# First block of a two-block model: projections, three attentions and the output projection as one interleaved stage

## The chip, the cores and the metric

One core of one Trainium2 chip runs the whole program. The time is the device time of one execution in microseconds (us), inputs in the chip's memory, output written back. The kernel before: 1134.98, 1138.11 and 1143.31 us in three runs, median 1138.11.

## What is computed

The program has two blocks on a sequence of 256 tokens, 1024 features, float32. The change is in the first block, whose attention has three kinds of heads on one projection, and, apart from that, in a triangular inverse of the second block. The 16 meta tokens stand ahead of the 256 (272 keys).

```python
h = concat([meta, pad, x])                       # 16 real meta rows, then 256 tokens
hn = rms_norm(h, attn_norm)
c_q, c_kv, k_rope, dq, dk, dv, sq, sk, sv = split(hn @ w_in)
# latent heads (mla, 6): q from rms_norm(c_q) @ w_qb, k and v from rms_norm(c_kv) @ w_kvb,
#   the last 32 of 96 query and key features rotated; plain causal softmax
# difference heads (dif, 4): two maps each, softmax(q1 k1 + bias) - lam * softmax(q2 k2 + bias),
#   then rms_norm over the head's 64 features
# window heads (swa, 6, two key heads): band of 128, bias, a sink in the softmax's sum
h = h + concat([y_mla, y_dif, y_swa]) @ w_out
h = h + (silu(rms_norm(h) @ w_gate) * (rms_norm(h) @ w_up)) @ w_down
```

The bias of the dif and swa heads is a table value of the distance query minus key (t5_bucket), the same for all pairs at one distance. The second block's gated delta rule needs the inverse of a unit triangular 128x128 matrix for 8 heads and 2 tiles, built up in 7 levels.

## The kernel before

All engines run one list of instructions each, in order, written out in `build`; semaphores tie them together. Nothing is scheduled by a planner: the order on an engine is the order of its block in the source.

**Weights.** They lie in memory as pieces (`PIECES`, most 128 x 1024 floats, 512 KB) in the order of use. SyncE loads piece i into one of 5 raw slots once piece i-5 has been split. ScalarE makes the first part of a piece (L1044, rounded to the matmul's fast format), VectorE the second (L1469, the remainder), into one of 6 slots; three matmuls (L472, L473, L474) then stand for one float32 product. Neither engine splits when it likes: `first_parts` and `second_parts` are called by `full` and `freed`, that is when the engine next waits for a bank of results, and go up to 4 pieces (`AHEAD`) beyond the piece that TensorE had taken when it closed that bank. The pieces "mla" are used whole, unsplit.

**Banks.** TensorE's results go to 8 PSUM banks in turn (`opened`), each used again when its reader has signalled.

**First block, in order on TensorE.** (1) 8 turns of the normed rows (transposes with `ident`, L490, L493), (2) two products "line0", "line1" (L614), which give for each of 10 bias heads the bias by distance, 2 x 399 values, (3) 13 pieces of features, 24 matmuls each (cq0, cq1, ckv, dq0, dq1, [sums of squares of the latents, L621 to L624], dk0, dk1, sq0, sq1, sq2, sk, krA, krB), (4) the values, 4 pieces, 72 matmuls, (5) the latent heads (L649 to L659): for each of 6 heads a product of 96 rows for the query and one of 32 rows for its swapped rotary part, both twice, and one for the key, (6) `attention(G1, {})` over 12 groups, (7) 8 turns of y, (8) the output projection, 2 halves of 4 pieces.

**Attention.** A group is a kind, a query tile and 2 to 4 heads; the list goes mla (4 heads), mla (2), dif, dif, swa, swa for query tile 0 and again for tile 1. TensorE writes scores one group ahead (`scores`, L532), transposes a group's probabilities (`turned`, L549, L558) and multiplies them with the values one group late (`weighted`, L580, L584). VectorE adds the bias and takes the maxima (`peaks_of`, L1546), for dif groups it subtracts the second map (`difference`, L1597 to L1604), and it finishes a group's output (`finish_one`); after a tile's dif groups it norms them (`sublayer_norm`, L1684 to L1687). ScalarE does the exponentials (L1086) and copies the transposed probabilities (`probs_out`, L1103, L1111). Its Ln and Exp for the latents' norm (L1163, L1165) need a table load each.

**Bias.** ScalarE copies the lines and writes them to memory 128 times over, once for each partition (L1144), so that GpSimd's five DMAs (L1391 to L1395) can read row q shifted by q: partition q starts at `P - 1 - q`. GpSimd waits for the whole write.

**Second block, levels** (`m`, `dx`, `dy`, L919, L933). In a level 1 to 6 TensorE multiplies M = LT_level X (4 banks of 4 products), ScalarE copies M, TensorE forms Y M ("dx") and M Y ("dy"), and VectorE subtracts them from X and Y (L1953); X is the transpose of Y. The last level has no dx.

The lines that set the order in the attention:

```python
def attention(G, between):
    scores(G[0])
    for i, g in enumerate(G):
        if i + 1 < len(G):
            scores(G[i + 1])
        for step in between.get(i, ()):
            step()
        turned(g)
        if i >= 1:
            weighted(G[i - 1])
    weighted(G[-1])
```

## Time and profile before

| what | value |
|---|---|
| median of three runs | 1138.11 us |
| the profiled execution | 1133.66 us, span 1131.8 us |
| TensorE (PE) busy | 1029.0 us, 91% |
| VectorE, ScalarE, GpSimd busy | 631.1, 497.0, 179.0 us |
| mean granted TensorE clock | 0.947 |
| DMA | 144.24 MB, 127 GB/s over the span |
| first block's attention part (to the output projection's end) | up to 217.7 us |

The span goes from the first to the last instruction of the profiled execution. A busy PE is not PE at its peak: matmuls overlap, and at the lower clock each is longer. Times of a row are from the span's start. Idle time of an engine is given in brackets with what ended it.

### The profile page before, as it was taken

What the parts mean: (1) busy time and instruction counts of PE and PEld (TensorE: products, weight loads), DVE (VectorE), ACT (ScalarE), POOL (GpSimd) and SP (SyncE); (2) the same over time, 40 slices, a digit from 0 to 9 for tenths busy, and PEclk for the clock granted to TensorE, in tenths of its full rate; (3) what the DMA queues carried; (4) which work ended last, traced back from release to release, by engine and by line L of the source; (5) the groups of instructions that cost most, each with busy time, mean ns of one, the idle gap of its engine ahead of it and who ended that gap; (6) DMA issues with size and microseconds to landing.
All of it is one profiled execution on the core that took longest, in us unless ns stands there. A gap on an engine that the chain in (4) does not pass through costs nothing. (4 is left out here: it accounts for less than half of the span.)

```text
span 1131.8 us, 16805 instructions
## 1 busy us (share of the span) xinstructions
PE 1029.0 (91%) x6524; PEld 916.0 (81%) x6524; DVE 631.1 (56%) x1293; ACT 497.0 (44%) x919; POOL 179.0 (16%) x129
## 2 busy tenths in 40 slices
PE   4779678899999979999899999899899998999998
PEld 2676467699999969879788888799888777988996
DVE  3244455655555567458756459635485665555443
ACT  4242444554444344453465653322244445444441
POOL 0001000000000004003644202154000001332231
PEclk9899788899999988989889898989999998999999
DMA  6766200545655543363522101200055443555641
GB/s 231 152 149 169 74 1 2 204 152 187 215 178 164 177 149 107 136 224 123 176 75 76 38 2 54 75 1 1 1 171 202 166 156 125 186 186 191 202 166 56
DMA packets 40089, 144.24 MB, mean 127 GB/s; under 512 B 4346, under 2 KB 4730, under 8 KB 40010
## 3 DMA queue, kind: packets, MB, share of 16 engines
q1 hardware_dynamic: 37328, 134.69, 35.6%
q10 hardware_dynamic: 2154, 6.64, 3.4%
q0 software_dynamic: 528, 1.84, 0.5%
q8 instruction: 52, 0.85, 0.3%
q14 instruction: 27, 0.22, 0.1%
HBM read 138.02 MB, written 5.13 MB: 126 GB/s over the span
## 5 line engine op out<-in xcount | busy, mean ns | idle before, releaser
L1469 DVE TENSOR_TENSOR parts<-raw,parts 128x1024 fp32r<-128x1024 f32 (+1 forms) x228 | 290.2, 1308 | 207.9 <-ACT parts L1044 206.6
L1044 ACT ACTIVATE parts<-raw 128x1024 fp32r<-128x1024 f32 (+1 forms) x228 | 231.0, 1050 | 161.3 <-PE psum L474 101.7
L472 PE MATMUL psum<-hT,parts 128*128 128x256 f32 (+1 forms) x936 | 270.1, 289 | 5.3 <-DVE parts L1469 5.3
L473 PE MATMUL psum<-hT,parts 128*128 128x256 f32 (+1 forms) x936 | 268.5, 287 | 0.0
L474 PE MATMUL psum<-hT,parts 128*128 128x256 f32 (+1 forms) x936 | 266.6, 285 | 0.0
L472 PEld LDWEIGHTS psum<-hT,parts 128*128 128x128 f32 x936 | 180.5, 193 | 8.9 <-issue 7.6
L474 PEld LDWEIGHTS psum<-hT,parts 128*128 128x128 f32 x936 | 181.3, 194 | 0.0
L473 PEld LDWEIGHTS psum<-hT,parts 128*128 128x128 f32 x936 | 180.7, 193 | 0.6
L472 PE MATMUL psum<-parts,arena_r 128*128 128x512 f32 x344 | 136.3, 396 | 0.6 <-DVE parts L1469 0.4
L474 PE MATMUL psum<-parts,arena_r 128*128 128x512 f32 x344 | 135.9, 395 | 0.0
L473 PE MATMUL psum<-parts,arena_r 128*128 128x512 f32 x344 | 135.9, 395 | 0.0
L1086 ACT ACTIVATE arena<-arena,npeaks 128x128 f32<-128x128 f32 (+4 forms) x136 | 55.9, 412 | 70.4 <-DVE npeaks L1566 52.8
L472 PE MATMUL psum<-parts,hT 128*128 128x512 f32 (+2 forms) x200 | 78.0, 390 | 6.5 <-DVE parts L1469 6.5
L472 PEld LDWEIGHTS psum<-parts,arena_r 128*128 128x128 f32 x344 | 64.5, 187 | 16.6 <-DVE parts L1469 0.8
L473 PE MATMUL psum<-parts,hT 128*128 128x512 f32 (+2 forms) x200 | 77.2, 386 | 0.0
L474 PEld LDWEIGHTS psum<-parts,arena_r 128*128 128x128 f32 x344 | 64.5, 187 | 15.7
L474 PE MATMUL psum<-parts,hT 128*128 128x512 f32 (+2 forms) x200 | 77.2, 386 | 0.0
L473 PEld LDWEIGHTS psum<-parts,arena_r 128*128 128x128 f32 x344 | 64.6, 188 | 15.0
L1401 POOL TENSOR_SCALAR arena<-cbuf 128x256 f32<-128x256 f32 x16 | 14.5, 910 | 324.6 <-DVE X L1737 323.5
L1437 POOL TENSOR_TENSOR arena<-arena 128x512 f32<-128x512 f32 x16 | 16.6, 1040 | 268.8 <-ACT arena_r L1372 268.8
L472 PEld LDWEIGHTS psum<-parts,hT 128*128 128x128 f32 x200 | 39.1, 195 | 14.5 <-issue 4.1
L1408 POOL CAST parts<-raw 128x1024 fp32r<-128x1024 f32 x20 | 22.0, 1098 | 181.5 <-PE psum L474 180.3
(281 smaller groups left out, 1424.5 us busy)
## 6 DMA issues: line engine op xcount, KB each, us to landing
raw<-weights SPq DMA_DIRECT2D x248, 512.0 KB, 4.2
lines<-arena ACTq DMA_DIRECT2D x1, 3990.0 KB
raw<-weights SPq DMA_DIRECT2D x4, 384.0 KB, 20.6
X<-x SPq DMA_DIRECT2D x2, 512.0 KB, 5.9
out<-X SPq DMA_DIRECT2D x2, 512.0 KB, 2.6
arena<-lines POOLq DMA_DIRECT2D x1, 768.0 KB, 8.2
arena<-consts ACTq DMA_DIRECT2D x1, 671.0 KB, 8.2
arena<-lines POOLq DMA_DIRECT2D x1, 544.0 KB, 5.8
```

The lines of the kernel that those rows point to most:

```text
L472: mm(ps, a, c, start=start, stop=False)
L473: mm(ps, a, d, start=False, stop=False)
L474: return mm(ps, b, c, start=False, stop=stop)
L1044: signal(A(split_slot(name)[0], whole_piece, ACT.Copy), "first_parts")
L1086: signal(A(map_slot(g, E, n), map_slot(g, S, n), ACT.Exp, bias=npeaks[:, col:col + 1], accum_out=sums[:, col:col + 1]), tag)
L1401: nc.gpsimd.tensor_scalar(al[:, h, :], cst("negdist"), slope, None, ALU.mult).then_inc(sem("alibi"), 1)
L1408: nc.gpsimd.tensor_copy(first, whole_piece).then_inc(sem("pool_first"), 1)
L1437: nc.gpsimd.tensor_tensor(v, v, v, ALU.mult).then_inc(sem("squares2"), 1)
L1469: signal(V_.tensor_tensor(second, whole_piece, first.bitcast(F32), ALU.subtract), "split_vector")
```

## The change

Five parts.

1. **Order of the first block.** Groups are sorted by kind: 4 dif, 4 swa, 4 mla. TensorE makes only dq and dk ahead of the attention; `between` then puts the values behind the scores of group 1, sq0 and sq1 behind those of group 2, and so on; the latent heads come at group 6, ahead of the mla groups. The columns of y and the rows of w_out are swapped so that the dif and swa heads are the first 5 of 8 feature tiles; these are turned at group 9 and the first half of the output projection's pieces runs at groups 10 and 11. ScalarE and VectorE follow in the same places (`early`, `extra1`).
2. **Start.** The lines' products go ahead of the transposes (and wait for the constants and "relneg", no longer for the norm), and their copies ahead of ScalarE's turned copies; `taken[0] = 1` lets the turned banks carry piece 1.
3. **Bias.** The lines are written to memory once (32 KB). The reads take row q shifted the other way, so queries stand in reverse order in their tile: `backwards` reverses them when ScalarE copies the projected queries, and `flip`, a matrix with ones on the other diagonal, puts y right when it is turned. cos and sin move into the constants that are loaded apart ("held").
4. **Rotary parts.** kr and its swapped form come from one piece, and each query head from one product of 128 rows; VectorE reads the swapped form from partitions 96 to 128.
5. **Levels.** Only Y is carried by products; X is the transpose of the new Y, copied by ScalarE.

```diff
+YM = (DH * DV + SH * SD) // P
-FEATURES1 = ["cq0", "cq1", "ckv", "dq0", "dq1", "dk0", "dk1", "sq0", "sq1", "sq2", "sk", "krA", "krB"]
+FEATURES1 = ["dq0", "dq1", "dk0", "dk1", "sq0", "sq1", "sq2", "sk", "cq0", "cq1", "ckv", "kr"]
...
+            return sorted(got, key=lambda g: ("dif", "swa", "mla").index(g["kind"]))
...
+        def backwards(ps):
+
+            src = ps[:, 0:SEQ]
+            return bass.AP(tensor=src.tensor, offset=src.offset + P - 1, ap=[src.ap[0], [P, TT], [-1, P]])
...
@@ block.tensor
             pe.wait_ge(sem("const_in"), 64)
+            pe.wait_ge(sem("relneg"), 1)
+            for v in range(2):
+                ps = opened(f"line{v}")
...
+            taken[0] = 1
             pe.wait_ge(sem("norm1"), 2)
...
-                for k in range(2):
-                    mm(ps[0:96, 0:SEQ], wq[h // 4][:, h % 4, k, 0:96], cn[:, k, real], start=(k == 0), stop=(k == 1))
-                for k in range(2):
-                    last = mm(ps[64:96, SEQ:2 * SEQ], wq[h // 4][:, h % 4, k, 96:128], cn[:, k, real], start=(k == 0), stop=(k == 1))
+                    for k in range(2):
+                        last = mm(ps[:, 0:SEQ], wq[h // 4][:, h % 4, k, :], cn[:, k, real], start=(k == 0), stop=(k == 1))
...
+            features("dq0", "dq1", "dk0", "dk1")
+            freed(pe, "p1_dq1")
+            freed(pe, "p1_dk1")
+            attention(G1, {0: [values, lambda: freed(pe, "vt_1")],
+                           1: [lambda: features("sq0", "sq1")],
+                           2: [lambda: features("sq2", "sk")],
+                           3: [lambda: features("cq0", "cq1")],
+                           4: [lambda: features("ckv", "kr")],
+                           5: [latent_sums],
+                           6: [latent_heads],
+                           9: [mixed_early],
+                           10: [lambda: out1_part(0, 0)],
+                           11: [lambda: out1_part(0, 1)]},
+                      {3: swa_heads, 7: mla_heads})
             freed(pe, "pv_" + G1[-1]["name"])
+            y_turns(range(YM, KD))
             for nh in range(2):
+                out1_part(1, nh)
...
-                    for what in (["dx", "dy"] if lv < LEVELS - 1 else ["dy"]):
...
+                    name = f"dy{lv}_{g}"
+                    ps = opened(name)
+                    for n in range(GH):
+                        s = slice(P * n, P * n + P)
+                        last = mm(ps[:, s], M[:, g, s], Yi[:, g, s], start=True, stop=True)
+                    closed(last, name)
+                for g in range(4 if lv < LEVELS - 1 else 0):
+                    name = f"x{lv}_{g}"
+                    ps = opened(name)
+                    freed(pe, f"dy{lv}_{g}")
+                    for n in range(GH):
+                        s = slice(P * n, P * n + P)
+                        last = nc.tensor.transpose(ps[:, s], Yi[:, g, s], ident)
+                    closed(last, name)
@@ block.scalar
-            act.dma_start(line_dram.rearrange("q h n -> h q n"),
-                          att1["PTm"][0:BH, 0:2 * LINE].unsqueeze(1).to_broadcast([BH, P, 2 * LINE])).then_inc(sem("lines_out"), 16)
+            act.dma_start(line_dram, att1["PTm"][0:BH, 0:2 * LINE]).then_inc(sem("lines_out"), 16)
+            turned_out(lambda k: f"h1_{k}", hT, ALL, lambda k: par("attn_norm")[:, k:k + 1])
...
+            attention(G1, {}, {0: values_out,
+                               1: lambda: swa_queries(0, 1),
+                               2: lambda: (swa_queries(2), swa_keys()),
+                               3: lambda: latents(0, 1),
+                               4: lambda: latents(2),
+                               5: latent_guess,
+                               6: latent_heads,
+                               9: lambda: mixed(range(YM))})
...
+                for g in range(4 if lv < LEVELS - 1 else 0):
+                    full(act, f"x{lv}_{g}")
+                    release(A(Xi[:, g, :], bank_of(f"x{lv}_{g}"), ACT.Copy), f"x{lv}_{g}")
@@ block.gpsimd
             def shifted(head0, heads, v, m0, n):
-                return bass.AP(tensor=line_dram.tensor, offset=head0 * 2 * LINE + v * LINE + m0 + P - 1,
-                               ap=[[BH * 2 * LINE - 1, P], [2 * LINE, heads], [1, n]])
+                return bass.AP(tensor=line_dram.tensor, offset=head0 * 2 * LINE + v * LINE + m0,
+                               ap=[[1, P], [2 * LINE, heads], [1, n]])
@@ block.vector
+            extra1 = {4: key_rotation, 5: latent_norm, 6: query_rotation,
+                      9: lambda: mixed_rest(range(YM)),
+                      10: lambda: residual([(t, 0, f"o10_0_{t}") for t in range(TT)], True),
+                      11: lambda: residual([(t, 1, f"o10_1_{t}") for t in range(TT)], True)}
+            dve.wait_ge(sem("dz_in"), 16)
             peaks_of(G1[0])
             for i, g in enumerate(G1):
+                if i == 3:
+                    dve.wait_ge(sem("sz_in"), 64)
                 if i + 1 < len(G1):
                     peaks_of(G1[i + 1])
                 if g["kind"] == "dif":
                     difference(g)
+                if i in extra1:
+                    extra1[i]()
                 if i >= 1:
                     if G1[i - 1]["kind"] == "swa":
                         sinks_in(G1[i - 1])
                     finish_one(G1[i - 1])
+                if i in (2, 4):
+                    sublayer_norm((i - 2) // 2)
```

`out1_part(half, nh)` makes half of the pieces of one half of the columns, with `split` and `three` as before. The order of the weight pieces in memory follows the new order of use.

TensorE where the attention begins, before: the last products of the latent heads (L659), scores of groups 0 and 1 (L532, 6 maps), transposes of group 0 (L549, L558).

```order
L659 MATMUL psum<-raw,arena 128x384 [waits bank1_free]
L659 MATMUL psum<-raw,arena 128x384 [waits bank2_free]
L532 MATMUL psum<-arena 128x144 [waits bank6_free,krot,bank2_free,bank3_free,bank7_free]
L532 MATMUL psum<-arena 128x144 x2
L532 MATMUL psum<-arena 128x144 [waits bank4_free]
L532 MATMUL psum<-arena 128x144 [waits bank5_free]
L532 MATMUL psum<-arena 128x144
L549 MATMUL psum<-cbuf,arena 16x128 [waits bank6_free,probs1]
```

The same engine now, from the end of the values at group 0 to the first product of sq0 at group 1 (L559, L568 are the transposes, L542 the scores, L482 to L484 a feature product).

```order
L484 MATMUL psum<-parts,hT 128x384
L559 MATMUL psum<-cbuf,arena 16x128 [waits bank1_free,differences,bank0_free]
L559 MATMUL psum<-cbuf,arena 16x128
L568 MATMUL psum<-cbuf,arena 128x128 [waits bank2_free]
L568 MATMUL psum<-cbuf,arena 128x128
L542 MATMUL psum<-arena 128x272 [waits bank3_free]
L542 MATMUL psum<-arena 128x272 [waits bank4_free]
L542 MATMUL psum<-arena 128x272 [waits bank5_free]
L542 MATMUL psum<-arena 128x272 [waits bank6_free]
L482 MATMUL psum<-hT,parts 128x256 [waits split_vector,bank7_free]
```

Between the scores of a group and its transposes there now stand the 48 matmuls of two features (or the values), where before there was at most the work of the neighbouring group.

ScalarE at the latents' norm, before: splits (L1044) and feature copies (L1159, L1168) around Ln and Exp.

```order
L1159 ACTIVATE arena<-psum 128x256 [waits bank6_full]
L1163 ACT_TABLE_LOAD
L1163 ACTIVATE arena<-arena 128x544 [waits lat_ms]
L1165 ACT_TABLE_LOAD
L1165 ACTIVATE arena<-arena 128x544 [waits lat_ln]
L1044 ACTIVATE parts<-raw 128x1024 [waits bank5_full,piece_in4]
L1168 ACTIVATE arena<-psum 128x272 [waits bank1_full]
```

And now, at group 5: exponentials of group 6 (L1154), Ln and Exp (L1253, L1255), then the probabilities of group 5 (L1171, L1179).

```order
L1154 ACTIVATE arena,sums<-arena,npeaks 128x272 [waits peak1]
L1154 ACTIVATE arena,sums<-arena,npeaks 128x272 x2
L1159 ACTIVATE difsum<-difsum 128x3 [waits sink_in]
L1253 ACT_TABLE_LOAD
L1253 ACTIVATE arena<-arena 128x544 [waits lat_ms]
L1255 ACT_TABLE_LOAD
L1255 ACTIVATE arena<-arena 128x544 [waits lat_ln]
L1171 ACTIVATE arena<-psum 16x384 [waits bank6_full,bank0_full]
```

The norm of the latents moved from among the features into the middle of the attention, where its neighbours on ScalarE are exponentials.

ScalarE at the output projection, before: turned copies of y (L1061), then seven splits in a row.

```order
L1061 ACTIVATE arena_r<-psum 128x256 [waits bank1_full]
L1061 ACTIVATE arena_r<-psum 128x256 [waits bank2_full]
L1044 ACTIVATE parts<-raw 128x1024 [waits bank0_full,piece_in1]
L1044 ACTIVATE parts<-raw 128x1024 [waits piece_used,piece_in2]
L1044 ACTIVATE parts<-raw 128x1024 [waits piece_used,piece_in3]
```

And now: the last turned copy of group 9 (L1129), probabilities of group 9 (L1171, L1179), exponentials of group 11 (L1154), and the first split behind them (L1112), which is that of out1_0.1.

```order
L1129 ACTIVATE arena_r<-psum 128x256 [waits bank1_full]
L1171 ACTIVATE arena<-psum 16x256 [waits bank2_full,bank0_full]
L1179 ACTIVATE arena<-psum 128x256 [waits bank3_full]
L1154 ACTIVATE arena,sums<-arena,npeaks 128x272 [waits peak1]
L1154 ACTIVATE arena,sums<-arena,npeaks 128x272
L1112 ACTIVATE parts<-raw 128x1024 [waits bank1_full,piece_in0,bank4_full]
L1112 ACTIVATE parts<-raw 128x1024 [waits bank6_full,piece_in1]
```

The splits of the output projection now follow exponentials and probability copies instead of the turned copies alone.

## Rows read from the trace of the kernel before

**Rows 1.** Busy time by stretches: length, PE, PEld, DVE, ACT, POOL, clock, DMA share, GB/s.
```profile
52.70:65.00 12.30, 12.29 (x98) 11.96 (x96) 3.59 (x5) 6.50 (x9) 0.00 (x0) 0.98 0.74 171
70.30:85.00 14.70, 13.60 (x96) 13.40 (x97) 4.40 (x4) 3.78 (x6) 0.00 (x0) 0.89 0.70 154
85.00:100.80 15.80, 13.09 (x72) 12.47 (x73) 5.54 (x7) 3.88 (x6) 4.68 (x5) 1.00 0.75 198
119.60:192.60 73.00, 53.31 (x321) 46.01 (x321) 34.05 (x174) 30.45 (x111) 0.00 (x0) 0.77 0.08 30
194.40:217.70 23.30, 22.94 (x98) 17.84 (x96) 16.90 (x20) 13.91 (x21) 0.00 (x0) 1.00 0.70 243
```

**Rows 2.** Waits, 0 to 120 us: engine, line waited for; total, times, longest.
```profile
ACT parts L1044 <- DMA raw<-weights: 50.2, 12, 15.0
```

**Rows 3.** Timeline, ScalarE's DMA queue and GpSimd: start, length, what, [idle before, releaser].
```profile
25.37 0.55 ACTq L1144 DMA_DIRECT2D lines<-arena  x1
...
95.53 0.97 POOL L1391 DMA_DIRECT2D arena<-lines  x1 [92.79 <-DMA lines<-arena]
```

**Rows 4.** DMA issues of the page: count, KB each, median us to landing.
```profile
raw<-weights SPq DMA_DIRECT2D x248, 512.0 KB, 4.2
lines<-arena ACTq DMA_DIRECT2D x1, 3990.0 KB
```

**Rows 5.** Timeline of TensorE: start and end of the first block's stretches.
```profile
24.68 0.59 PE L472 MATMUL psum<-hT,parts 128*128 128x272 f32 x1
...
50.19 1.25 PE L621 MATMUL psum<-arena,ones 128*128 128x272 f32 x2 [8.47 <-ACT arena L1152]
...
70.30 0.55 PE L472 MATMUL psum<-hT,parts 128*128 128x256 f32 x1 [5.31 <-DVE parts L1469]
...
223.00 3.65 PE L493 MATMUL psum<-cbuf,arena 128*128 128x128 f32 x16 [5.29 <-DVE arena L1520]
```

**Rows 6.** Timeline of TensorE in the attention, groups dif0_0 and dif0_2.
```profile
128.65 0.39 PE L580 MATMUL psum<-arena 128*128 128x128 f32 x2
...
132.89 0.60 PE L549 MATMUL psum<-cbuf,arena 128*16 128x128 f32 x2 [3.17 <-DVE arena L1604]
```

**Rows 7.** Timeline of TensorE in the latent heads.
```profile
109.78 1.05 PE L651 MATMUL psum<-arena,raw 128*32 128x256 f32 x4
...
112.39 1.05 PE L651 MATMUL psum<-arena,raw 128*32 128x256 f32 x4
113.37 0.67 PE L654 MATMUL psum<-arena,raw 128*64 128x272 f32 x2
```

**Rows 8.** Timeline of VectorE: a split and the latent norm.
```profile
59.50 1.23 DVE L1469 TENSOR_TENSOR parts<-raw,parts 128x1024 fp32r<-128x1024 f32 x1 [3.69 <-ACT parts L1044]
...
61.94 0.44 DVE L1650 TENSOR_SCALAR arena<-arena 128x544 f32<-128x544 f32 x1 [0.52 <-DVE arena L1647]
...
67.69 1.32 DVE L1657 SCALAR_TENSOR_TENSOR arena<-arena,pbuf 128x272 f32<-128x272 f32 x3
```

**Rows 9.** Timeline of ScalarE: the latent norm's first guess, and a split.
```profile
63.10 1.28 ACT L1165 ACT_TABLE_LOAD   x1
64.39 0.66 ACT L1165 ACTIVATE arena<-arena 128x544 f32<-128x544 f32 x1
64.95 1.04 ACT L1044 ACTIVATE parts<-raw 128x1024 fp32r<-128x1024 f32 x1
```

**Rows 10.** Timeline of VectorE: first and last of the sublayer norm's 15 instructions.
```profile
186.70 0.43 DVE L1684 TENSOR_TENSOR scr<-arena 128x256 f32<-128x256 f32 x1
...
189.86 0.42 DVE L1687 TENSOR_TENSOR arena<-arena,st 128x256 f32<-128x256 f32 x1
```

**Rows 11.** Timeline of TensorE: transposes ahead of the levels, and one level's first products.
```profile
730.83 1.04 PE L906 MATMUL psum<-cbuf,arena 128*128 128x128 f32 x8
...
750.78 3.74 PE L919 MATMUL psum<-arena 128*128 128x128 f32 x32
```

**Rows 12.** Timeline of VectorE: a level's first subtraction.
```profile
755.45 0.69 DVE L1953 TENSOR_TENSOR arena<-arena,psum 128x512 f32<-128x512 f32 x1 [3.78 <-PE psum L933]
```

More of the change, by code:

```diff
@@ new lines, in _, with y_turns @@
+            y = att1["y"].rearrange("p (t n) -> p t n", t=TT)
+            tiles2 = [slice(P * t, P * t + P) for t in range(TT)]
+            flip = cst("flip")
+            def y_turns(ks):
+                for k in ks:
+                    name = f"yT1_{k}"
+                    ps = opened(name)
+                    for t in range(TT):
+                        last = nc.tensor.transpose(ps[:, P * t:P * t + P], y[:, t, P * k:P * k + P], flip if k < YM else ident)
+                    closed(last, name)
+                    arrivals[k] = name
@@ new lines, in out1_part @@
+            def out1_part(half, nh):
+                for t in range(TT):
+                    opened(f"o1{half}_{nh}_{t}")
+                for j in (2 * half, 2 * half + 1):
+                    name = f"out1_{nh}.{j}"
+                    w = [h.rearrange("p (k n) -> p k n", k=2) for h in split(name)]
+                    for t in range(TT):
+                        job = f"o1{half}_{nh}_{t}"
+                        for k in range(2):
+                            need(2 * j + k)
+                            last = three(bank_of(job), [yT[:, s, 2 * j + k, tiles2[t]] for s in range(2)],
+                                         [h[:, k, :] for h in w], j == 2 * half and k == 0, j == 2 * half + 1 and k == 1)
+                        if j == 2 * half + 1:
+                            closed(last, job)
+                    if j == 2 * half + 1:
+                        piece_used[name] = f"o1{half}_{nh}_1"
+                    else:
+                        done_with(name, last)
@@ new lines, in queries, with values_out @@
+            def queries(dst, what, c, scale):
+                full(act, f"p1_{what}{c}")
+                release(A(dst[:, c, :].rearrange("p (t n) -> p t n", t=TT), backwards(bank_of(f"p1_{what}{c}")), ACT.Copy,
+                          scale=scale), f"p1_{what}{c}")
+            def values_out():
+                for t, rows in (("m", META), (0, P), (1, P)):
+                    full(act, f"vt_{t}")
+                    ti = 0 if t == "m" else t + 1
+                    release(A(V[0:rows, ti, 384:768], bank_of(f"vt_{t}")[0:rows, 0:384], ACT.Copy), f"vt_{t}")
@@ new lines, in swa_queries, with swa_keys, latent_guess @@
+            def swa_queries(*cs):
+                for c in cs:
+                    queries(sQ, "sq", c, SD ** -0.5)
+            def swa_keys():
+                full(act, "p1_sk")
+                release(A(one["sKT"], bank_of("p1_sk")[:, 0:ALL], ACT.Copy), "p1_sk")
+            def latent_guess():
+                act.wait_ge(sem("lat_ms"), 1)
+                signal(A(rs[:, 1:3, :], rs[:, 1:3, :], ACT.Ln), "lat_ln")
+                act.wait_ge(sem("lat_ln"), 1)
+                signal(A(rs[:, 1:3, :], rs[:, 1:3, :], ACT.Exp, scale=-0.5), "lat_guess")
```

337 lines of the change are left out of this document (160 added, 177 removed).

## The prediction, made before the changed kernel ran

> **What bounds the kernel now.** I read the busy time by stretches first [rows 1], then who waits for whom [rows 2], the two ends of the DMA that this points at [rows 3], the DMA issues [rows 4] and TensorE's timeline [rows 5, 6]. In a projection stretch TensorE is busy without a gap: 12.29 us for 98 matmuls, 0.1255 us each. In the attention it is busy for 53.3 of 73.0 us, at a granted clock of 0.77 [rows 1]. The attention thus loses 19.7 us to waits, and more to the clock.
>
> Ahead of the attention it is mostly the weights. In the first 120 us ScalarE waited 50.2 us for raw pieces, in 12 waits [rows 2]. From 25.4 to 95.5 us the DMA of "lines" was under way [rows 3]; it writes 3990 KB where a piece has 512 KB, and over the whole program a piece lands in 4.2 us (median) [rows 4]. TensorE stood 8.5 us at 50.19, 5.3 us at 70.30 [rows 5] and 2.7 us in the value stretch (15.8 less 13.1) [rows 1]. The first and the last I put down to the lines DMA; the second is VectorE, whose split stood behind its latent norm.
>
> In the attention a group's transposes wait for VectorE's `difference` (3.17 us at 132.89), and the waits keep the clock low: two 128-column instructions take 0.39 us at 128.65 and 0.60 us at 132.89, behind the wait [rows 6]. These are the 2.4 and the 1.2 GHz level.
>
> **The sum, first block.** It ends with the last matmul of the output projection, at 223.00 less 5.29, 217.7 us; its projections begin at 24.68 [rows 5]: 193.0 us. TensorE's work in it at the full clock: 13 feature pieces at 24 x 0.1255 = 3.0, 39.0; values 12.8 (of the 13.1); sums of squares 1.3; latent heads 18.8 (six of 2.61, 109.78 to 112.39 [rows 7], and a tail of 3.1); attention 53.3 x 0.77 = 41, taken as 40; turns of y 1.8; output projection 22.6 [rows 1]. Together 136.3. Waits 8.5, 5.3, 2.7, 19.7: 36.2. The rest, 20.5, is low clock and handing over.
>
> Now the new order, term by term.
>
> Start: the bias-line matmuls go ahead of the transposes, into the time in which TensorE waits for the first norm, and cost nothing there. But ScalarE and VectorE now split four more pieces ahead of the first turn of h (1.04 and 1.23 us each [rows 8, 9]). The projections start at 23.0, 1.7 earlier. The constants must be there about 1 us earlier than now; if they are not, that 1 us goes.
>
> Work: krA and krB become one piece, -3.0. Each query head loses its second pair of products, 0.98 us (112.39 to 113.37 [rows 7]), x 6 = -5.9. Left 127.4; the first 20 matmuls stay at the low clock, +2.1.
>
> Waits. Handing over to the first scores 0.8; banks and value copies at group 0, 1.0. At groups 0 to 4 the values or two features (6.0 us) stand between the next group's scores and this group's transposes. VectorE needs there four peaks, a difference and two splits, some 7 us, TensorE's iteration is 8 to 9: these waits vanish, but for 1.3 at group 3, where the first sublayer norm (186.70 to 190.28, 3.6 us [rows 10]) stands ahead of the peaks.
>
> The worst place is the latent norm. VectorE comes to it behind the key rotation, a finish, the second sublayer norm (3.6) and three peaks. From its third line (61.94) to its last product (69.01) it took 7.1 us [rows 8], with two table loads on ScalarE inside [rows 9]. Walking through: the last feature ends at 85.4, VectorE is at that third line at 95.5, the norm is there at 103; TensorE has transposes, weighted sums and one group's scores, until 93.5. Wait 9.5.
>
> The Trainium skill says (ScalarE: Activation LUTs, What ACT_TABLE_LOAD costs) that a switch of tables takes about 2.66 us with its drain. Here the load took 1.28 us and the Exp followed at once (63.10, 64.39) [rows 9], so the row stands; by the page the wait, and the time, would be up to 2.8 us longer.
>
> Groups 7 and 8 have no filler, but as mla groups no difference either: 0.5. In the output projection's first quarter (group 10) piece out1_0.1 is split only behind the exponentials of group 11, since ScalarE splits ahead only when it comes to a later bank. TensorE is through its first 12 matmuls (2.8 us) 9.5 us after it began group 10's scores; ScalarE has ten copies and six exponentials to do until 11.8, then 1.04, and VectorE 1.23: 14.3. Wait 4.8. At the end three turns of y wait for the last finish, 1.2. Waits together: 0.8 + 1.0 + 1.3 + 9.5 + 0.5 + 4.8 + 1.2 = 19.1.
>
> Clock and handing over were 20.5, with a wait every 7 to 8 us. After there are two long waits; the stretch behind the wait of 5.3 us had 14.7 us at 0.89 [rows 1], 1.6 lost. I take 6.4. Bounds: 3 (two such stretches) and 20.5.
>
> The bias reads fetch the same bytes, from 32 KB in place of 4 MB; the first is needed at 38 and its source is out by about 20. Copying PSUM backwards, five times, is nowhere in the trace: the nearest is any copy of that size, part of ScalarE's rows; between no change and twice the time it is hidden behind features, but for the last, below 1 us. I take nothing.
>
> New length: 127.4 + 2.1 + 19.1 + 6.4 = 155.0, end at 178.0, 39.7 earlier. Bounds: with the old clock loss and a third more waits 19.2 (39.7 - 14.1 - 6.4); with half the waits and the low bound of the clock 52.6.
>
> **The sum, triangular levels.** TensorE is dense here: 16 products (32 half products in the row) take 3.74 us at 750.78, 3.57 without the tail [rows 11], a level of 48 products 10.7. Five levels lose 16 products each and get 16 transposes, of which eight took 1.04 with their tail, 0.9 without [rows 11]: 1.8. Gain 1.78 x 5 = 8.9, if the longer chain (product, VectorE's subtraction of 0.69 us [rows 12], transpose, ScalarE's copy, next product) stays hidden. A subtraction ends 1 us behind its product, and the transposes of the groups before cover that; a level has four copies more on ScalarE and four subtractions less on VectorE. Bounds 0 and 8.9.
>
> Sum: 48.6. The profiled execution took 1133.66 (span 1131.8), so 1085; the runs shown have the median 1138.11, 4.5 above it. I forecast 1087.
>
> **The rivals.**
> 1. ScalarE and VectorE take the weights' place. Both do exponentials, splits and copies in order; if the first seven groups keep a wait like the 3.17 us beside the 19.1, that is some 20 us: 1107. For it: those waits were for VectorE. Against: in the attention it had nothing to do for half of the time.
> 2. The long waits come out at half, 9.5 less, with 2.5 less of clock: 1075.
> 3. The clock falls in the levels, because a row of transposes stands in each. Then each loses about 1.6 us as behind the wait at 70.30, and the gain is gone: 1095. For it: 16 transposes behind a wait took 3.65 us (223.00) [rows 5]; against it: eight between products took 1.04 (730.83) [rows 11], the fast pace. The Trainium skill speaks for it (TensorE: Matmul & The Clock Gate, Part 4: PE-mode transpose): transposes do not count as busy in the same way as matmuls.
> 4. The lines DMA is not what delays the weights. Then each piece is late by 50.2 / 12 = 4.2 us again. But TensorE now wants 27 pieces in 155 us, one in 5.7, not one in 3.0, so only the first few are missed, some 8 us: 1095.
> 5. Slower: the waits between fillers stay just frequent enough, and the whole interleaved stage runs at 1.2 GHz. Its 115 us of work doubles: 1087 + 115 - 6 = 1196. It decides from a granted clock of 0.70: 115 x (1/0.70 - 1) = 49 us eats the gain. The attention of now had 0.77, with its pauses; the pauses would have to stay.
>
> **How the numbers follow.** Forecast 0.60; rival 1 0.18; rival 2 0.10; rival 3 0.05; rival 4 0.04; rival 5 0.03. From the median the bounds of gain, 19.2 and 61.5, are 1119 and 1077. The range leaves out rival 5 and the far end of rival 1: 1070 to 1110. A measurement here tells about 1% (11 us) from no change. All but rival 5 are faster by over 1%: faster 0.95, 0.03 within 1% (rival 5 in part of the stage), slower 0.02.
>
> **What would show it.** Right: the lines DMA lands within a few us; ScalarE waits below 15 us for raw pieces in the first block; norm2's transposes start near 183 in place of 223.0; one wait of 8 to 11 us ahead of the first latent head, one of 3 to 6 in the first quarter of the output projection; a granted clock over 0.9 between 40 and 170; a level of 8.9 us without gaps. Wrong: waits of 3 us at each of groups 0 to 4, a level that stays near 10.7, a low clock between fillers, or pieces that come late as before.

## The result and the profile after

The changed kernel took 1083.69 us (median of four runs, 1079.46 to 1085.53) beside 1137.23 us before; the ratio is 0.952, 95% interval 0.949 to 0.955. It is 53.5 us faster, where 51 was forecast. The profiled execution took 1079.46 us, span 1077.6; TensorE is busy for 997.3 us, 93% of it.

The first block ends at 175.53 less 5.30, 170.2 us, where it ended at 217.7 [rows 5]: 47.5 us earlier, where 39.7 were forecast. TensorE's timeline after:

```profile
23.13 0.55 PE L482 MATMUL psum<-hT,parts 128*128 128x256 f32 x1 [0.55 <-DVE hT L1580]
...
104.44 2.04 PE L666 MATMUL psum<-arena,raw 128*128 128x256 f32 x4 [9.15 <-DVE arena L1754]
...
175.53 3.65 PE L503 MATMUL psum<-cbuf,arena 128*128 128x128 f32 x16 [5.30 <-DVE arena L1614]
```

The busy time by stretches, with the columns of [rows 1], answers to the attention's row there (53.31 busy of 73.00, clock 0.77):

```profile
23.13:38.27 15.14, 14.61 (x97) 14.42 (x97) 6.13 (x14) 4.55 (x10) 0.80 (x1) 1.00 0.86 274
38.27:53.27 15.00, 13.65 (x88) 13.14 (x88) 8.52 (x28) 8.68 (x23) 0.00 (x0) 1.00 0.50 170
53.27:95.30 42.03, 41.90 (x322) 38.23 (x322) 28.75 (x105) 19.18 (x58) 0.00 (x0) 1.00 0.13 43
95.30:104.44 9.14, 0.00 (x1) 0.04 (x1) 4.58 (x11) 5.58 (x11) 0.00 (x0) 0.61 0.00 0
104.44:134.13 29.69, 28.70 (x166) 20.90 (x166) 15.57 (x62) 16.50 (x54) 0.00 (x0) 0.95 0.20 72
140.40:170.20 29.80, 29.33 (x152) 23.82 (x152) 18.47 (x26) 13.27 (x22) 0.00 (x0) 0.94 0.50 164
```

From 53.27 to 95.30 TensorE works through feature pieces and attention groups at the full clock and is idle for 0.13 us. Then it stands still for 9.14 us. (In the first row the clock reads 1.00, yet TensorE starts its first 27 matmuls, to 29.0, only every 0.21 us, and one every 0.12 us from there; the kernel before begins in the same way, with 20 matmuls. The column does not show this.) What TensorE waited for, 20 to 180 us (the row of hT holds 0.55 us at the block's start and 0.73 behind its end; the 5.3 are behind its end too):

```profile
PE psum L666 <- DVE arena L1754: 9.1, 1, 9.1
PE psum L503 <- DVE arena L1614: 5.3, 1, 5.3
PE psum L482 <- DVE parts L1563: 2.2, 1, 2.2
PE psum L482 <- DVE hT L1580: 1.3, 2, 0.7
PE psum L542 <- DVE arena_r L1580: 1.0, 1, 1.0
PE psum L482 <- DVE peaks L1640: 0.8, 1, 0.8
PE psum L559 <- ACT arena L1241: 0.6, 1, 0.6
PE psum L542 <- issue: 0.5, 1, 0.5
PE psum L687 <- DVE arena L1678: 0.5, 1, 0.5
```

Inside the block that is 14.7 us (9.1 + 2.2 + 1.0 + 0.8 + 0.6 + 0.5 + 0.5). The DMA side: GpSimd's wait for the lines, and ScalarE's whole wait for raw pieces up to 180 us:

```profile
19.68 0.97 POOL L1485 DMA_DIRECT2D arena<-lines  x1 [16.93 <-DMA lines<-arena]
```
```profile
ACT parts L1112 <- DMA raw<-weights: 2.5, 1, 2.5
```

The lines are out at 19.7 in place of 95.5 [rows 3], and the 50.2 us of ScalarE's waits for weights [rows 2] are 2.5. A level of the triangular stage, from one start of its products to the next (699.02 to 707.91), takes 8.89 us and has no gap; with its row of transposes the granted clock is 1.00:

```profile
699.02 3.74 PE L993 MATMUL psum<-arena 128*128 128x128 f32 x32
702.59 1.91 PE L1001 MATMUL psum<-cbuf,arena 128*128 128x128 f32 x16
704.34 3.74 PE L985 MATMUL psum<-arena 128*128 128x128 f32 x32
707.91 3.74 PE L993 MATMUL psum<-arena 128*128 128x128 f32 x32
```
```profile
699.02:747.06 48.04, 48.04 (x434) 1.00 0.01 2
```

From span to span of the two profiled executions the change gives 54.2 us: 47.5 in the first block, 9.1 in the levels (from the stage's start to the matmuls behind it 64.7 before, 55.6 after), and 2.4 are given back in between, where no instruction changed. What gives them back is below.

### The profile page after: what moved, and what is told of

It reads as the page before. It is cut to its first block and busy times, and to the rows that moved or that the text cites. A ratio compares the mean times of both kernels' runs of the same rounds, so it can differ in the third digit from the quotient of the medians.

```text
span 1077.6 us, 16556 instructions
## 1 busy us (share of the span) xinstructions
PE 997.3 (93%) x6396; PEld 890.4 (83%) x6396; DVE 618.3 (57%) x1276; ACT 504.6 (47%) x938; POOL 178.1 (17%) x129
## 3 DMA queue, kind: packets, MB, share of 16 engines
q1 hardware_dynamic: 37184, 134.17, 37.3%
## 5 line engine op out<-in xcount | busy, mean ns | idle before, releaser
L1563 DVE TENSOR_TENSOR parts<-raw,parts 128x1024 fp32r<-128x1024 f32 (+1 forms) x227 | 289.0, 1310 | 177.7 <-ACT parts L1112 176.4
L1112 ACT ACTIVATE parts<-raw 128x1024 fp32r<-128x1024 f32 (+1 forms) x227 | 229.5, 1048 | 111.6 <-PE psum L484 101.7
L482 PE MATMUL psum<-hT,parts 128*128 128x256 f32 (+1 forms) x928 | 267.6, 288 | 1.3 <-DVE hT L1580 1.3
L484 PE MATMUL psum<-hT,parts 128*128 128x256 f32 (+1 forms) x928 | 264.8, 285 | 0.0
L482 PEld LDWEIGHTS psum<-hT,parts 128*128 128x128 f32 x928 | 179.1, 193 | 5.1 <-DVE hT L1580 2.3
L484 PEld LDWEIGHTS psum<-hT,parts 128*128 128x128 f32 x928 | 180.2, 194 | 0.0
L482 PE MATMUL psum<-parts,arena_r 128*128 128x512 f32 x344 | 137.0, 398 | 2.3 <-DVE parts L1563 2.2
L484 PE MATMUL psum<-parts,arena_r 128*128 128x512 f32 x344 | 136.5, 397 | 0.0
L1154 ACT ACTIVATE arena<-arena,npeaks 128x128 f32<-128x128 f32 (+4 forms) x136 | 55.9, 412 | 68.6 <-DVE npeaks L1660 48.5
L482 PE MATMUL psum<-parts,hT 128*128 128x512 f32 (+2 forms) x200 | 78.8, 394 | 3.4 <-DVE parts L1563 2.7
L482 PEld LDWEIGHTS psum<-parts,arena_r 128*128 128x128 f32 x344 | 64.7, 188 | 18.8 <-DVE parts L1563 2.6
L484 PE MATMUL psum<-parts,hT 128*128 128x512 f32 (+2 forms) x200 | 78.1, 391 | 0.0
L483 PE MATMUL psum<-parts,hT 128*128 128x512 f32 (+2 forms) x200 | 78.1, 390 | 0.0
L484 PEld LDWEIGHTS psum<-parts,arena_r 128*128 128x128 f32 x344 | 64.8, 188 | 15.8
L1504 POOL TENSOR_TENSOR parts<-raw,parts 128x1024 fp32r<-128x1024 f32 x20 | 49.3, 2464 | 1.6
## 6 DMA issues: line engine op xcount, KB each, us to landing
arena<-lines POOLq DMA_DIRECT2D x1, 768.0 KB, 10.7
```

The costliest lines, as they stand in the source:

```text
L482: mm(ps, a, c, start=start, stop=False)
L483: mm(ps, a, d, start=False, stop=False)
L484: return mm(ps, b, c, start=False, stop=stop)
L1112: signal(A(split_slot(name)[0], whole_piece, ACT.Copy), "first_parts")
L1154: signal(A(map_slot(g, E, n), map_slot(g, S, n), ACT.Exp, bias=npeaks[:, col:col + 1], accum_out=sums[:, col:col + 1]), tag)
L1504: nc.gpsimd.tensor_tensor(second, whole_piece, first.bitcast(F32), ALU.subtract)\
```

## The experiments

Medians are compared. The runs were made on three chips, and the kernel before ran beside each group of them, with medians of 1136.23, 1135.50 and 1136.66 us; a run's ratio is to the kernel before beside it. Where only a part of the program is in question, the end of the first block is read, which is where TensorE begins its last wait for the second norm.

**The levels alone, on the kernel before.**

```diff
-  for what in (["dx", "dy"] if lv < LEVELS - 1 else ["dy"]):
-      ...
-      a, b = (Yi, M) if what == "dx" else (M, Yi)
-      last = mm(ps[:, s], a[:, g, s], b[:, g, s], start=True, stop=True)
+  last = mm(ps[:, s], M[:, g, s], Yi[:, g, s], start=True, stop=True)
...
+  for g in range(4 if lv < LEVELS - 1 else 0):
+      ...
+      last = nc.tensor.transpose(ps[:, s], Yi[:, g, s], ident)
```

The text on record has the edit the wrong way round: the product and the subtraction go, the transposes and copies come, as in the change.

> The kernel before with the changed levels alone: the first levels' second matrix is brought up to date by a product and a subtraction instead of 16 transposes and four copies in a stage of their own. My theory (TensorE runs these stages without a wait, so each level is as long as its matmuls): the seven levels of one chain shrink by 8.9 us, as the sum in the prediction had it, so about 1128 us, ratio about 0.992. A rival: part of the gain stood beside other engines' work and comes back as waits of TensorE for the subtractions on VectorE; then 0 to 4 us are gained, ratio 0.997 to 1.000. A second rival, that transposes in the levels had the clock lowered: then more than 8.9, with the granted clock of that stretch higher than before.

Measured: 1126.95 us, ratio 0.991 (0.989 to 0.993), 9.3 us less.

```profile
747.13 3.74 PE L924 MATMUL psum<-arena 128*128 128x128 f32 x32
...
756.02 3.74 PE L924 MATMUL psum<-arena 128*128 128x128 f32 x32
```

8.89 us a level here too. From the last transposes ahead of the levels to the matmuls behind them it takes 56.0 us where it took 64.7: 8.7 of the sum's 8.9. No wait for VectorE's subtractions comes, and the clock of the stretch is 1.00.

**The lines written once, on the kernel before.**

```diff
-  act.dma_start(line_dram.rearrange("q h n -> h q n"), ...to_broadcast([BH, P, 2 * LINE]))
+  act.dma_start(line_dram, att1["PTm"][0:BH, 0:2 * LINE])
-  offset=... + m0 + P - 1, ap=[[BH * 2 * LINE - 1, P], ...]
+  offset=... + m0, ap=[[1, P], ...]
```

The run leaves out the reversed order of the queries that goes with this read, so each pair gets the bias of the mirrored distance; it serves for its time alone.

> The kernel before, with the bias lines written to memory once (32 KB instead of 4.2 MB) and each key's read shifted the other way, so that the bias of a pair is taken from the mirrored distance: this part of the computation is changed, its instructions and their number on the compute engines are the same. My theory (the lines' 4.2 MB take the DMA engines from the weights, so that TensorE waits at 50.2 for a weight piece): the 8.5 us wait there goes, the short ones around it too, and the write on the lines no longer takes tens of us; in all 8 to 14 us less, about 1123 to 1129 us, ratio 0.988 to 0.993. The 5.3 us wait at 70.3 (latent norm on VectorE) stays. The rival of the prediction (the wait has another cause: splitting, or the order of the queue): the 8.5 us stay, and the time is within 2 us of before, ratio 0.998 to 1.002.

Measured: 1116.22 us, ratio 0.981 (0.977 to 0.985): 20.0 us less, more than I expected. TensorE's waits ahead of the attention, first of the kernel before (20 to 118 us), then of this one (20 to 100 us):

```profile
PE psum L472 <- DVE parts L1469: 9.1, 4, 5.3
PE psum L621 <- ACT arena L1152: 8.5, 1, 8.5
```
```profile
PE psum L532 <- issue: 0.7, 1, 0.7
```

All 17.6 us are gone, the 5.3 at 70.30 [rows 5] with them, which I had expected to stay. VectorE still does the latent norm behind the same splits, but in front of it it no longer waits for weights: it is through the norm 8.5 us after TensorE begins dk0 (51.2 and 42.7), where it took 16.3 (69.0 and 52.7). The pieces split ahead of the norm last TensorE 12.3 us from dk0 on. The attention starts 21.8 us earlier (97.83 for 119.63) and gives 3.8 of it back: with the same work its clock is 0.71 where it was 0.77.

```profile
97.80:174.50 76.70, 57.48 (x320) 0.71 0.08 28
```

The first block ends at 199.7, 18.0 earlier.

**The stages apart again, on the changed kernel.**

```diff
-  attention(G1, {0: [values, ...], 1: [features("sq0", "sq1")], 2: ..., 6: [latent_heads], ...})
+  features(all); latent_sums(); values(); latent_heads()
+  attention(G1, {output projection's first half at groups 10 and 11 only})
```

> The changed kernel with the first block's stages apart again: all projections, the latent sums, the value products and the latent heads ahead of the first attention group; the lines written once, the merged products and the changed levels stay. By my theory (the matmuls put between the groups fill the waits of about 3 us a group and with them the clock stays high): the waits come back, 2.5 to 3.2 us at each of 9 or 10 groups, the clock in the attention falls under 1.00, and the time is 20 to 35 us longer, 1104 to 1119 us. By the rival that the lines and the merged products brought the first block's gain: 0 to 8 us longer, up to 1092 us. If the waits come back and the clock stays, the difference is the sum of the waits less the latent wait of 9.15 us.

Measured: 1100.47 us, 16.8 more than the changed kernel: between the two expectations, nearer to the first. TensorE's waits for the probabilities are back, five of 1.9 to 5.5 us where nine or ten of about 3 were expected (20 to 157 us, the first two rows of the view), and the clock of the attention is 0.76:

```profile
PE psum L557 <- DVE arena L1696: 18.1, 4, 5.5
PE psum L557 <- ACT arena L1151: 1.9, 1, 1.9
```
```profile
87.10:157.00 69.90, 46.99 (x281) 0.76 0.09 31
```

The block ends at 187.5. Its waits are 24.2 us (18.1, 1.9, two below 1 us, and 2.6 at the output projection) against 14.7: 9.5 of the 17.3 us are waits, 0.7 is the start (23.79), and the other 7.1 are what is left, the clock and handing over together. Interleaving fills some 19 us of waits and pays 9.15 of them back at the latent norm, which costs nothing with the stages apart.

**3990 KB (4.1 MB; 4.2 MB in the texts on record) written beside the changed kernel's lines, and nothing waits for them.**

```diff
+  act.dma_start(line_dram[1:P + 1]..., cbuf[0:BH, 0:2 * LINE]...to_broadcast([BH, P, 2 * LINE]))
```

> The changed kernel with a second write of 4.2 MB to memory behind that of the lines, from constants, which nothing waits for until the program's end: the DMA engines' load of before without its dependency. If the load on the DMA engines is what held the weights up: their pieces of the first 60 us land in 10 us and more instead of 4.7 us in the median, TensorE waits for a piece or its split again between 25 and 60 us, and the time is 5 to 11 us longer, 1089 to 1095 us. If it was the wait for the lines' own landing (the reads behind it): the pieces may be late, but no wait of TensorE grows and the time stays within 2 us of 1083.7.

Measured: 1102.07 us, 18.4 more; twice what I expected, and partly by another way. TensorE at the attention's start, VectorE there, and ScalarE's waits up to 120 us:

```profile
48.53 1.34 PE L542 MATMUL psum<-arena 32*128 32x144 f32 x16 [10.87 <-issue]
```
```profile
42.62 1.83 DVE L1566 TENSOR_TENSOR parts<-raw,parts 128x768 fp32r<-128x768 f32 x2 [15.60 <-DMA arena<-lines]
```
```profile
ACT parts L1113 <- DMA raw<-weights: 26.8, 7, 10.0
```

The weights are late again (26.8 us of waits for 2.5; the 512 KB pieces of the first 60 us land in 20.0 us in the median, for 4.7), and so is the bias read (the largest lands in 33.0 us, for 10.7), which VectorE awaits for 15.6 us with the splits queued behind it. TensorE pays 10.9 us, and 3.3 at 68.90. The load alone takes 17.2 us of the first block.

**The lines of before in the new order.**

```diff
-  act.dma_start(line_dram, att1["PTm"][0:BH, 0:2 * LINE])
+  act.dma_start(line_dram.rearrange("q h n -> h q n"), ...to_broadcast([BH, P, 2 * LINE]))
-  ap=[[1, P], ...]
+  ap=[[BH * 2 * LINE + 1, P], ...]
```

> The changed kernel with the lines written as in the kernel before: 128 copies (4.2 MB), of which each partition reads its own, so that the bias reads wait for the whole write. With the load alone, unwaited, 18.4 us were lost. My theory now: in the new order the first attention group needs the bias at 38 us, so the write's whole length lies on the path. In the kernel before the write took 70 us beside the weights; here it starts at about 15 us, and with a read of 8 us behind it the first scores' peaks come at 75 to 95 in place of 38: 40 to 57 us more, 1124 to 1140 us, so that the whole gain of the change is gone. Rival: the write is fast once the weights have filled their buffers and stand still; then 20 to 30 us more, 1104 to 1114.

Measured: 1139.69 us, ratio to the kernel before 1.002 (1.000 to 1.005): the whole gain of the change, levels included, is gone.

```profile
93.86 0.66 PE L482 MATMUL psum<-parts,hT 128*128 128x384 f32 x1 [46.44 <-DVE peaks L1641]
```
```profile
85.29 0.97 POOL L1486 DMA_DIRECT2D arena<-lines  x1 [82.55 <-DMA lines<-arena]
```

The write runs from 16.88 to 85.3, and the first peaks wait for it. In the old order that wait lay behind 95 us of projections; in the new one the bias is needed at 38.

**Two products a query head again, on the changed kernel.**

```diff
-  mm(ps[:, 0:SEQ], wq[...][:, h % 4, k, :], ...)
+  mm(ps[0:96, 0:SEQ], wq[...][:, h % 4, k, 0:96], ...)
+  mm(ps[64:96, SEQ:2 * SEQ], wq[...][:, h % 4, k, 96:128], ...)
```

> The changed kernel with the query heads' two products apart again, as in the kernel before: twelve short matmuls more in the six latent heads, all else as changed. By the sum in the prediction TensorE is the bound in this stretch (0.98 us a head from a row): 5.9 us more, about 1090. Rival: in the interleaved stage TensorE waits behind the heads for VectorE or ScalarE anyway, so that a part of it is hidden: 0 to 3 us more.

Measured: the first block ends at 181.65 less 5.30, 176.4, that is 6.1 later (5.9 by the sum). TensorE's waits are those of the changed kernel (9.1, 2.1, 1.0, 0.8 us), so none of the work is hidden, as the rival would have it. The median is 1086.58 us, only 2.9 more, which by itself is within the rival's 0 to 3; by the ratios to the kernel before (0.957 and 0.952) it is some 5 us, and its profiled execution is 10.7 above the changed kernel's. The part behind the block, in which nothing differs, makes these numbers uncertain by several us (last section), so that I go by the block.

**Three edits against the waits that are left.** First each alone: the second sublayer norm from group 4 to group 7; the latent heads one place later on TensorE and ScalarE, with VectorE's query rotation behind the finish of the group before.

```diff
-  if i in (2, 4): sublayer_norm((i - 2) // 2)
+  if i in (2, 7): sublayer_norm(i // 4)
```
```diff
-  6: [latent_heads], ...   {3: swa_heads, 7: mla_heads}
+  {3: swa_heads, 7: lambda: (latent_heads(), mla_heads())}
```

> The changed kernel with the second sublayer norm (3.6 us on VectorE) moved from group 4 to group 7 of the attention, behind the latent norm and the query rotation. My theory: VectorE is what the wait of 9.15 us at 104.44 is for, and all that stands in its queue ahead of the latent norm counts in full; the wait falls by 3.6 to 5.5 us, and as the 3.6 us then stand where VectorE has time, the whole time falls by 3 to 4 us, to about 1080. Rival: the norm only delays VectorE while it would wait anyway (for ScalarE's copies of the features, or for TensorE's last feature); then the wait stays at 8 to 9 us and the time is 1083 to 1084. Rival: it turns up again as a wait at groups 7 or 8; then the latent wait falls and another of 2 to 4 us appears.

> The changed kernel with the latent heads one place later on TensorE (behind group 6's own scores, weighted sums and transposes instead of ahead of them), so that TensorE has that work to do while the latent norm is made. My theory: the wait falls by the work that is put ahead of it, 2.3 to 3.3 us, to 6 to 7 us; in all 2 to 3 us less, about 1081. Rival: the work that is moved needed the same engines' results, so it waits as long itself; then the sum of the waits between 95 and 110 us is as before, and the time is 1083 to 1084.

Measured: 1082.19 and 1082.85 us. In the traces the latent wait, first of the norm's run, then the waits in its place with the heads later (95 to 110 us):

```profile
PE psum L666 <- DVE arena L1754: 5.6, 1, 5.6
```

```profile
PE psum L568 <- ACT arena L1170: 3.5, 1, 3.5
PE psum L666 <- DVE arena L1676: 1.0, 1, 1.0
PE psum L559 <- ACT arena L1153: 0.9, 1, 0.9
```

The norm stood in full in VectorE's way: 9.15 less 5.59 is 3.6, its own length [rows 10]. The heads' edit leaves 5.4. The first block ends 2.8 and 2.2 us earlier; the medians fall by only 1.5 and 0.8, less than the runs of one kernel differ among themselves, and the ratios to the kernel before, 0.953 both, do not fall at all (0.952 for the changed kernel).

> The changed kernel with both edits (second sublayer norm at group 7, latent heads one place later), and the piece out1_0.1 split early, at group 8, on ScalarE and VectorE. If each wait is what its row says, the latent wait falls from 9.15 to about 3, the wait of 2.15 us in the output projection's first quarter goes, and the granted clock behind the latent wait (0.90) rises: 7 to 9 us less, about 1076. Rival: the gains overlap, since the same engine (VectorE) is late behind both; then 3 to 5 us less, 1079 to 1081.

Measured: 1079.22 us, 4.5 less, where the rival had it. The latent wait is 2.3, the 2.2 of the output projection is gone, and a new one stands at the turns of y, behind the early split (127.67):

```profile
127.67 1.35 PE L687 MATMUL psum<-cbuf,arena 128*128 128x128 f32 x10 [3.15 <-issue]
```

So three versions were timed side by side on one chip: both edits without the early split, the changed kernel, and all three edits.

> The changed kernel with the second sublayer norm at group 7 and the latent heads one place later, without the early split of out1_0.1. In the run with all three edits the early split took away the wait of 2.15 us in the output projection but a wait of 3.15 us stood at the turns of y (127.67), behind that split on ScalarE and VectorE. If that is its cause, the 2.15 us are back, the 3.15 us gone or below 1, and the first block ends about 1 us earlier than with three edits, at 163 to 164.5; the whole time within 2 us of 1079. If the wait at the turns of y is not the split's, it stays, and the block ends 2 us later than with three edits.

> The changed kernel itself once more, to be compared on the same chip with the versions with two and with three edits: 1083.7 us, between 1079 and 1086. If the remainder of the program behind the first block can be 901 us as well as 908 us long with the same instructions, its profiled execution may show either.

> The version with three edits once more, beside the changed kernel on the same chip. If its gain is that of the first block (5.5 us there), it is 3 to 5.5 us under the changed kernel, 1078 to 1081; if the first run's gain was chance between chips, the two are within 1.5 us.

Measured, six runs each: two edits 1077.53 us (1071.18 to 1080.65), changed kernel 1083.52 (1075.75 to 1085.58), three edits 1078.95 (1075.78 to 1081.45). The ratios to the kernel before are 0.947 (0.943 to 0.951), 0.952 (0.948 to 0.956) and 0.948 (0.945 to 0.952). Without the early split the wait at the turns of y is gone and the 2.2 back, as the first case had it, but the block ends at 165.6, with the split at 164.5: the split is worth 1 us there and nothing in the time. Two edits are 6.0 us below the changed kernel, three 4.6; the intervals overlap, so that both are likely faster and not proven so. That the latent wait falls is in the traces, from 9.15 to 3.3 (two rows, with two edits, 90 to 104 us):

```profile
PE psum L666 <- DVE arena L1676: 2.3, 1, 2.3
PE psum L568 <- ACT arena L1170: 0.9, 1, 0.9
```

The changed kernel's own block ended at 168.9 in this second run, 1.3 earlier than in the first; differences of blocks are no surer than that, the split's 1 us among them. Beside this run the blocks of two and three edits end 3.3 and 4.4 us earlier.

## Why the prediction was right

*Start.* 23.13 for 23.0; the constants came in time.

*Work.* The query heads' 5.9 us are 6.1 (two products apart). The krA and krB term of 3.0 was not tried alone.

*Waits, 19.1 forecast, 14.7 found.* The latent norm was walked through almost to the row: VectorE at its third line at 95.52 (95.5 forecast), the last product out at 104.2 (103), TensorE there at 95.3 (93.5), wait 9.15 (9.5). That the wait itself is so close is in part luck, since the last two were both late, by 1.2 and 1.8:

```profile
95.52 0.44 DVE L1747 TENSOR_SCALAR arena<-arena 128x544 f32<-128x544 f32 x1
...
100.24 0.72 DVE L1593 TENSOR_TENSOR arena<-arena 128x544 f32<-128x544 f32 x1 [4.28 <-ACT arena L1255]
...
102.85 1.32 DVE L1754 SCALAR_TENSOR_TENSOR arena<-arena,pbuf 128x272 f32<-128x272 f32 x3
```

Of the smaller terms, group 3's 1.3 does not exist, and the last turns' is 0.5 for 1.2. The output projection's is 2.2 for 4.8: the piece is split behind the exponentials of group 11, as forecast, but it is out 12.5 us after the start of group 10's scores (140.4 and 127.8) for 14.3, and TensorE comes for it after 10.4 for 9.5. Of the waits this is the term that missed most; the rest is 2.9 (1.3, 0.6, 1.0) for 2.3.

*The table load.* The norm took 8.65 us from its third line, where [rows 8] had 7.1. ScalarE's rows tell why:

```profile
96.29 1.28 ACT L1253 ACT_TABLE_LOAD   x1
97.58 0.66 ACT L1253 ACTIVATE arena<-arena 128x544 f32<-128x544 f32 x1
98.25 1.28 ACT L1255 ACT_TABLE_LOAD   x1
99.55 0.66 ACT L1255 ACTIVATE arena<-arena 128x544 f32<-128x544 f32 x1
```

It comes out of the exponentials only at 96.29, so the first load, too, stands behind VectorE's line (over at 95.96): 1.6 us that the walk did not have. Each load is 1.28 us and the next instruction follows at once; the drain of the Trainium skill (ScalarE: Activation LUTs, What ACT_TABLE_LOAD costs) does not show.

*Clock and handing over, 6.4 forecast.* 147.1 us of length less 129.5 of work (the forecast's own, with its 2.1 for the start) and 14.7 of waits leaves 2.9. Once the waits every 7 to 8 us are gone, the clock stays up: 1.00 over the 66 us from 29.0 to the latent wait, then 0.95 over 29.7 us and 0.94 over the last 29.8. By these shares the last two stretches lose 3.3 us, about what is left. The misses in the waits and in the clock, 4.4 and 3.5, are the 7.8 us by which the first block beat its sum.

*The levels.* 8.9 forecast, 9.3 by the run with them alone, 8.89 a level. Rival 3 fell: the stage with a row of 16 transposes in each level runs at clock 1.00, and a transpose takes 0.11 us in such a row. The rule of the Trainium skill that I had weighed for it (TensorE: Matmul & The Clock Gate, Part 4: PE-mode transpose) did not decide here: either these fp32 transposes do count as busy, or the 64 product instructions beside every 16 of them keep the clock up without their help. No run here tells which.

*Where the reading was wrong.* The step "the first and the last I put down to the lines DMA; the second is VectorE" failed. All the waits ahead of the attention, 17.6 us, were the lines', the 5.3 at 70.30 too. VectorE's norm stood in front of the split in its queue, but was only late there because the weights had come late; the releaser named by the row was the last of a chain and not its cause. The sum did not suffer, since it struck out all the old waits together and built new ones, but rival 4's price did: "some 8 us" for late pieces in the new order, where the load alone costs 18.4 and the load with its dependency 56. It counted the weights and left out the bias reads, which move from 95 us to 38.

*The other rivals, and the total.* Rival 1 fell: between 53.27 and 95.30 no group has a wait like the 3.17 us. So did rival 2: of the two long waits only the shorter came out at half (2.2 for 4.8, 9.15 for 9.5). So did rival 5, with the clock above. The sum of 48.6 us became 54.2 from span to span: 7.8 more in the first block, 0.2 more in the levels, and 2.4 given back behind the block, for which it had no term. That two misses stand against each other, and that the forecast of 51 lies above its own sum, makes 1087 for 1083.69 closer than the sum deserves.

*Shares.* Of 53.5 us, the levels are 9.3 (alone, on before). The lines alone on before give 20.0, and undone on after they cost 56: they and the new order are not a sum, the second can't be had without the first. Stages apart cost 16.8.

*What was given back.* Behind a wait of 7.65 us in the unchanged second block the low clock lasted longer, first before, then after (length, busy, clock, DMA share, GB/s):

```profile
421.70:441.70 20.00, 19.97 (x132) 0.74 0.18 55
```
```profile
374.90:394.90 20.00, 19.97 (x96) 0.51 0.09 27
```

From the end of that wait to the next 512-column product it takes 27.6 us where it took 23.4: 4.2 us of the gain go, of which others return a part. It is hardly chance. Over the 20 us behind this wait the clock is 0.73 or 0.74 in all three traces built on the kernel before (before, levels alone, lines once) and 0.51 to 0.54 in all eleven built on the changed kernel. Nor is it the interleaving or the small write of the lines: the runs with the stages apart (0.52) and with the lines of before (0.53) are among the eleven, and levels or lines alone on the kernel before do not bring it. Which of the other parts does, and by what way, stays open.

## What to carry to other kernels

A filler between dependent groups pays twice, in the waits that it fills and in the clock that then stays up; here 9.5 us net of waits and some 7 for clock and handing over together. Before moving a stage forward, list every DMA that it needs and when each can have landed: a transfer that was hidden behind the old order (68 us of a broadcast write) can eat the whole gain, and the edit that makes it small belongs to the same change. And a wait named after an engine is to be followed to that engine's own wait before it is called that engine's.

## What the runs showed of the hardware

*The same program, two lengths.* The changed kernel and its second run, the same file, have the same wait of 1.37 us at the same instruction, and behind it one runs on at the full clock and the other at the low one. First after, then after again:

```profile
601.65 1.09 PE L568 MATMUL psum<-cbuf,arena 128*128 128x128 f32 x8 [1.37 <-ACT arena L1154]
```
```profile
600.76 1.97 PE L568 MATMUL psum<-cbuf,arena 128*128 128x128 f32 x8 [1.37 <-ACT arena L1154]
```
```profile
600.00:610.00 10.00, 8.63 (x62) 1.00 0.01 2
```
```profile
600.00:610.00 10.00, 9.23 (x40) 0.53 0.01 2
```

Between two instructions that stand on either side (561.73 to 653.22, and 560.76 to 657.32) this is 5.1 us. From the second norm to the end the program with the changed levels took 901.2 to 908.5 us in twelve traces (902.1 and 908.4 for the same file). So an edit of 3 us in the first block can show 1 us in the median, as the norm's did, or twice itself, as the two edits' did (3.3 and 6.0); such an edit is judged by its waits, and only one of some 10 us by the time. The Trainium skill (TensorE: Matmul & The Clock Gate, Part 1: The HAM clock gate) says that the stretch at the low clock at a kernel's start differs from run to run; here it differs behind waits in the middle too.

*The broadcast write was slow by itself.* In the last run with it, from 60 to 84 us, it is the only transfer (queue: packets, MB, share of 16 engines):

```profile
q10 hardware_dynamic: 372, 1.19, 46.9%
```

1.19 MB in 24 us is 50 GB/s, and a packet of 3.2 KB held an engine for 0.48 us (0.469 x 16 x 24 / 372); over the changed kernel a packet of the weights' queue, 3.6 KB, held one for 0.17 (37.3% of 16 x 1077.6 us by 37184). The Trainium skill (DMA: Bandwidth & Descriptors, Why a DMA increments its semaphore by 16 and not by 1) states that such a DMA is spread over the largest number of engines up to 16 that divides the slowest dimension of both its sides, which is 10 heads here; the share of 0.47 is below 10 of 16, which agrees as far as it goes. Why each packet is slow was not tried.
